# Row statistics: the squares of the last two tiles summed by TensorE instead of GpSimd, and the last output tile in two column halves

## What is computed

```python
def rmsnorm(x, w):
    xf = x.astype(jnp.float32)
    y = xf * lax.rsqrt(jnp.mean(xf * xf, axis=-1, keepdims=True) + EPS)
    return y.astype(x.dtype) * w
...
    for l in range(DEPTH):
        h = rmsnorm(x, norm_w[l])
        proj = h @ w_in[l]
...
        x = x + merged @ w_out[l]
    return rmsnorm(x, final_norm_w)
```

## Time and profile before

| | us |
|---|---|
| median of 3 runs | 3040.17 |
| lowest, highest | 3035.26, 3040.46 |
| span of the profiled execution | 3039.6 |
| TensorE busy in it | 2960.4 (97%) |
| VectorE, ScalarE, GpSimd busy | 1725.0, 1422.3, 421.7 |

### The profile page before, as it was taken

The page is one execution under the profiler, slowest core; times in us unless marked ns, Lnnn a source line. Parts: engine busy times, 40 slices in busy tenths (PEclk is TensorE's granted clock), DMA queues, the critical chain, the costliest instruction groups (busy, mean ns, idle before and its releaser), DMA issues. The chain is left out here.

```text
span 3039.6 us, 51611 instructions
## 1 busy us (share of the span) xinstructions
PE 2960.4 (97%) x20584; PEld 2383.2 (78%) x20584; DVE 1725.0 (57%) x2616; ACT 1422.3 (47%) x2795; POOL 421.7 (14%) x282
## 2 busy tenths in 40 slices
PE   9999989999999999999999999999999999999999
PEld 7788768777787878778777777778888877788887
DVE  7766742677437676733767445554444455554444
ACT  4555542666434555533666345763232356633322
POOL 1554510000013445400000020000000100000000
PEclk9999999999999999999999999999999999999999
DMA  4121112221222112112121222213222221122222
GB/s 151 64 83 59 51 59 89 73 75 60 84 88 98 64 64 85 42 66 91 60 74 60 106 87 87 77 49 111 97 97 97 84 87 62 51 98 98 95 97 83
DMA packets 42688, 243.17 MB, mean 80 GB/s; under 512 B 6832, under 2 KB 7792, under 8 KB 17136
## 3 DMA queue, kind: packets, MB, share of 16 engines
q1 hardware_dynamic: 42480, 240.30, 22.4%
HBM read 233.36 MB, written 2.20 MB: 77 GB/s over the span
## 5 line engine op out<-in xcount | busy, mean ns | idle before, releaser
L319 PE MATMUL bank<-hT,ws 128*128 128x512 f32 x2112 | 873.5, 414 | 12.7 <-issue 7.2
L323 PE MATMUL bank<-hT,ws 128*128 128x512 f32 x2112 | 827.5, 392 | 0.0
L322 PE MATMUL bank<-hT,ws 128*128 128x512 f32 x2112 | 825.9, 391 | 0.0
L319 PEld LDWEIGHTS bank<-hT,ws 128*128 128x128 f32 x2112 | 398.2, 189 | 96.9 <-issue 18.5
L276 DVE TENSOR_TENSOR ws<-raw,ws 128x2048 fp32r<-128x2048 f32 x160 | 372.7, 2330 | 164.7 <-ACT ws L270 161.6
L323 PEld LDWEIGHTS bank<-hT,ws 128*128 128x128 f32 x2112 | 397.3, 188 | 87.3
L270 ACT ACTIVATE ws<-raw 128x2048 fp32r<-128x2048 f32 x172 | 328.8, 1912 | 290.8 <-PE bank L319 175.5
L322 PEld LDWEIGHTS bank<-hT,ws 128*128 128x128 f32 x2112 | 399.0, 189 | 68.1 <-issue 1.4
L1113 PE MATMUL bank<-uS,ws 128*128 128x512 f32 x512 | 199.2, 389 | 0.0
L1116 PE MATMUL bank<-uS,ws 128*128 128x512 f32 x512 | 199.2, 389 | 0.0
L1117 PE MATMUL bank<-uS,ws 128*128 128x512 f32 x512 | 199.2, 389 | 0.0
(11 more groups left out here) (382 smaller groups left out, 4859.2 us busy)
## 6 DMA issues: line engine op xcount, KB each, us to landing
raw<-in_w_ff SPq DMA_DIRECT2D x64, 1024.0 KB, 4.7
raw<-in_w_delta SPq DMA_DIRECT2D x32, 1024.0 KB, 4.7
raw<-in_w_diff SPq DMA_DIRECT2D x32, 1024.0 KB, 4.7
raw<-in_w_att SPq DMA_DIRECT2D x20, 1024.0 KB, 4.8
raw<-in_w_merge_a SPq DMA_DIRECT2D x16, 1024.0 KB, 4.8
raw<-in_w_merge_b SPq DMA_DIRECT2D x16, 1024.0 KB, 4.8
raw<-in_w_out SPq DMA_DIRECT2D x16, 1024.0 KB, 4.8
rows<-sum_rows SPq DMA_DIRECT2D x16, 512.0 KB, 5.6
```

The lines of the kernel that those rows point to most:

```text
L319: first = pe.matmul(out, hi, x[:, 0, k], start=(begin and k == steps[0]), stop=False)
L322: pe.matmul(out, hi, x[:, 1, k], start=False, stop=False)
L323: last = pe.matmul(out, lo, x[:, 0, k], start=False, stop=(end and k == steps[-1]))
```

## The change

The square of tile 6 gets a buffer of its own (`sq[:, 2]`), and so does that of tile 7 (`sq[:, 3]`). GpSimd adds tiles 1 to 5 only (`GATHERED` = 6). `gathered_sum` sums `sq[:, 0]` as before and then tile 6's square, by two more matmuls. The last tile of `k.xT` is made, added and squared in two column halves: TensorE runs its product twice over 256 columns, into two banks (`last_half`, `LAST_BANKS_FF`), and VectorE adds each half as it is done. In the last feed-forward panel of either layer it is the same, and at the kernel's end the last tile is written out by two transfers. With two norms, the gate weights' raw copy moves to another buffer, since the squares now need its place.

```diff
+GATHERED = KT - 2
+SQUARES = 4
 class RowTotals(RowStats):
...
-    def square(self, act, t):
-        if t >= 2:
+    def square(self, act, t, added=None, before=0):
+        if 2 <= t < GATHERED:
             act.wait_ge(self.gathered, t - 1)
-        for part in HALVES if t == KT - 1 else (slice(0, SEQ),):
-            act.activation(self.sq[:, min(t, 1), part], self.k.xT[:, t, part], ACT.Square,
+        for j, part in enumerate(HALVES) if t == KT - 1 else ((0, slice(0, SEQ)),):
+            if added is not None:
+                act.wait_ge(added, before + t + 1 + j)
+            act.activation(self.sq[:, min(t, 1) + max(t + 1 - GATHERED, 0), part], self.k.xT[:, t, part], ACT.Square,
                            scale=1.0 if self.gain is None else self.gain[:, t:t + 1]).then_inc(self.squared, 1)
...
-        for t in range(1, KT - 1):
+        for t in range(1, GATHERED):
             self.gather_one(pool, t)
...
     def gathered_sum(self, pe):
-        pe.wait_ge(self.gathered, KT - 2)
+        pe.wait_ge(self.gathered, GATHERED - 1)
         for j, part in enumerate(HALVES):
             pe.matmul(self.half(j), self.k.ones, self.sq[:, 0, part], start=True, stop=False)
+        pe.wait_ge(self.squared, KT - 1)
+        for j, part in enumerate(HALVES):
+            pe.matmul(self.half(j), self.k.ones, self.sq[:, 2, part], start=False, stop=False)
...
             pe.wait_ge(self.squared, KT + j)
-            pe.matmul(self.half(j), self.k.ones, self.sq[:, 1, part], start=False, stop=True).then_inc(self.summed, 1)
+            pe.matmul(self.half(j), self.k.ones, self.sq[:, 3, part], start=False, stop=True).then_inc(self.summed, 1)
...
-    def square(self, act, t):
-        self.first.square(act, t)
+    def square(self, act, t, added):
+        self.first.square(act, t, added)
         if t == 0:
...
     def gather(self, pool):
-        for t in range(1, KT - 1):
+        for t in range(1, GATHERED):
             self.first.gather_one(pool, t)
...
                 pe.wait_ge(self.added, n - banks[n - 1::-1].index(banks[n]))
-            whole(st.product(pe, k.bank[banks[n]][:, :], c, h, self.aS)).then_inc(self.tile, 1)
+            if n < KT - 1:
+                whole(st.product(pe, k.bank[banks[n]][:, :], c, h, self.aS)).then_inc(self.tile, 1)
+                continue
+            for j, part in enumerate(HALVES):
+                if j:
+                    pe.wait_ge(self.added, KT - 2)
+                whole(st.product(pe, self.last_half(j), c, h, self.aS[:, :, :, part])).then_inc(self.tile, 1)
+    def last_half(self, j):
+        return self.k.bank[self.banks[(KT - 1, KT - 3)[j]]][:, HALVES[j]]
...
         def square(n):
-            act.wait_ge(self.added, n + 1)
             if self.unscaled:
+                act.wait_ge(self.added, n + 1 + n // (KT - 1))
                 self.unscaled.high(act, n)
-            stats.square(act, n)
+            stats.square(act, n, self.added)
         act.preload_act_table_set(LN_EXP)
...
         def add(n):
-            dve.wait_ge(self.tile, n + 1)
-            dve.tensor_tensor(k.xT[:, n], k.xT[:, n], k.bank[self.banks[n]][:, :], ALU.add).then_inc(self.added, 1)
+            for j, part in enumerate(HALVES) if n == KT - 1 else ((0, slice(0, SEQ)),):
+                dve.wait_ge(self.tile, n + 1 + j)
+                dve.tensor_tensor(k.xT[:, n, part], k.xT[:, n, part], self.last_half(j) if n == KT - 1 else k.bank[self.banks[n]][:, :], ALU.add).then_inc(self.added, 1)
             if self.unscaled:
...
-    out = OutStage(k, st, following, aS, sq[:, 0:2], banks + banks, left, pairs, gate_weights, late=True)
+    out = OutStage(k, st, following, aS, sq[:, 0:SQUARES], banks + banks, left, pairs, gate_weights, late=True)
     fn_loaded, = k.sems("final_gain_loaded")
-    norms = TwoNorms(k, out.stats, gain, fn_loaded, sq[:, 2:4], 6)
+    norms = TwoNorms(k, out.stats, gain, fn_loaded, sq[:, SQUARES:2 * SQUARES], 6)
     with k.nc.Block() as block:
...
+LAST_BANKS_FF = (7, 3)
 OUT_BANKS_FF = (0, 1, 2, 3, 6, 2, 3, 6)
...
         rr = k.sb(ctx, "row_scale", [P, SEQ], F32)
-        stats = RowTotals(k, k.sb(ctx, "sq", [P, 2, SEQ], F32), 0) if following else None
+        stats = RowTotals(k, k.sb(ctx, "sq", [P, SQUARES, SEQ], F32), 0) if following else None
         with nc.Block() as block:
...
                     for n in range(KT):
-                        sp.wait_ge(added, nth(NP - 1, 8, n + 4))
-                        sp.dma_start(result[:, n], k.xT[:, n]).then_inc(stored, 16)
-                    sp.wait_ge(stored, 16 * KT)
+                        for j, part in enumerate(HALVES) if n == KT - 1 else ((0, slice(0, SEQ)),):
+                            sp.wait_ge(added, nth(NP - 1, 8, n + 4 + j))
+                            sp.dma_start(result[:, n, part], k.xT[:, n, part]).then_inc(stored, 16)
+                    sp.wait_ge(stored, 16 * (KT + 1))
...
-                    def step(kk, n):
+                    def step(kk, n, part=slice(0, SEQ), bank=None):
                         if kk == 0:
...
                             pe.wait_ge(added, nth(i, 8, (c - 2) * 4 + n))
-                        o = k.bank[4 + n][:, :]
+                        o = k.bank[4 + n if bank is None else bank][:, part]
                         hi, lo = (w[:, kk, n * P:(n + 1) * P] for w in wv)
-                        first = pe.matmul(o, hi, uS[:, 0, kk], start=(kk == 0), stop=False)
+                        first = pe.matmul(o, hi, uS[:, 0, kk, part], start=(kk == 0), stop=False)
                         if kk == 0 and n == 0:
                             first.then_inc(st.slot_free, 1)
-                        pe.matmul(o, hi, uS[:, 1, kk], start=False, stop=False)
-                        last = pe.matmul(o, lo, uS[:, 0, kk], start=False, stop=(kk == 3))
+                        pe.matmul(o, hi, uS[:, 1, kk, part], start=False, stop=False)
+                        last = pe.matmul(o, lo, uS[:, 0, kk, part], start=False, stop=(kk == 3))
                         if kk == 3:
...
                     if last_panel and c == 3:
-                        for n in range(4):
+                        for n in range(3):
                             for kk in range(4):
                                 step(kk, n)
+                        for j, part in enumerate(HALVES):
+                            if j:
+                                pe.wait_ge(relu, 4 + 4 * NP)
+                            for kk in range(4):
+                                step(kk, 3, part, LAST_BANKS_FF[j])
                         if stats:
...
                     last.then_inc(tile, 1)
-                pe.wait_ge(out.added, KT)
+                pe.wait_ge(out.added, KT + 1)
                 inner(0, 1)
...
                                 act.wait_ge(added, nth(i, 8, n + 4))
-                                stats.square(act, n)
+                                if n < KT - 1:
+                                    stats.square(act, n)
+                                else:
+                                    stats.square(act, n, added, nth(i, 8, 4) - 1)
                                 if n == 4:
...
                     for n in range(4 * (c - 2), 4 * (c - 1)):
-                        dve.wait_ge(otile, nth(i, 8, n))
-                        dve.tensor_tensor(k.xT[:, n], k.xT[:, n], k.bank[4 + n % 4][:, :], ALU.add).then_inc(added, 1)
+                        for j, part in enumerate(HALVES) if last and n == KT - 1 else ((0, slice(0, SEQ)),):
+                            dve.wait_ge(otile, nth(i, 8, n + j))
+                            dve.tensor_tensor(k.xT[:, n, part], k.xT[:, n, part], k.bank[LAST_BANKS_FF[j] if last and n == KT - 1 else 4 + n % 4][:, part], ALU.add).then_inc(added, 1)
                         if last and following and n == 5:
...
```

More of the change, by code:

```diff
@@ L1006, in _ @@
             norms.vector(dve, rows)
-            dve.wait_ge(out.added, KT)
+            dve.wait_ge(out.added, KT + 1)
     k.next_phase()
@@ L3450, in build @@
                         if more:
[L3451 removed]
+                            out_phase(k, s_out, s_next, mS, macc[:, 0:SQUARES], OUT_BANKS_MERGE, KT - 1, [(pA, a["pA"][l + 1])],
                                       weights(split, a["gA"], l + 1))
@@ L3456, in build @@
                         first_split = split_area(yS, NGATE)
-                        raw = Carve(macc[:, 4], F32)(KT, NGATE)
+                        raw = Carve(k.cb[:, CB_N:], F32)(KT, NGATE)
                         last_out_phase(k, s_out, s_next, mS, macc, OUT_BANKS_MERGE, KT - 1, a["fn"], gain, pB[:, 0, PB_N1:PB_N1 + KT],
@@ L3477, in build @@
                     k.sb(two, "before_uS", [P, 32 if more else 128], F32)
-                    out_ff_phase(k, s_out, yS, k.sb(two, "sq", [P, 2, SEQ], F32), OUT_TILE[TILES - 1],
+                    out_ff_phase(k, s_out, yS, k.sb(two, "sq", [P, SQUARES, SEQ], F32), OUT_TILE[TILES - 1],
                              s_ff, s_next, lambda t, l=l: pB[:, l, PB_N2 + t:PB_N2 + t + 1],
```

1 line of the change is left out of this document (removed).

## The result

The changed kernel takes 3042.70 us (median of 13 runs, 3037.79 to 3044.72), the kernel before 3036.54 us (13 runs, 3034.20 to 3040.86, among them the three shown ahead of the prediction). The ratio is 1.0016, 95% interval [1.0009, 1.0024]: 0.16% slower, within the 0.2% that the prediction calls no change. Eleven more runs (e10) beside 27 more of before gave 3042.14 against 3039.46 us, ratio 1.0012 [1.0003, 1.0022].

What follows compares the result with a forecast made beforehand. TensorE's queue, 97% busy, was taken as the bound. Terms 0.63 + 2.02 + 2.34 - 0.37 - 0.22 = +4.40 us on 3040.17 gave 3044.6 us, 0.14% slower; range 3037.8 to 3048.5 us.

Steps and rivals of the forecast that it cites:

- D: End of layer 0's feed-forward part: the 1.1 us GpSimd stall goes, passes take back two thirds; -0.37 us.
- The price of a half-width matmul: Each 256-column matmul of the last tile's product: 0.120 us, bounded below by 0.112 us from idle products.
- w: Time added to a projection's last-tile product by making it as 48 half-width matmuls: +0.32 us.
- A: End of block 1's output projection, layer 0: last sums start later, TensorE not ready for early squares; +0.63 us.
- B: End of block 1's output projection, layer 1, two norms: eight passes added to a full queue; +2.02 us.
- C: Block 2's output projection, layer 0: four more passes and a longer product in a full queue; +1.17 us.
- E: Block 2's output projection, layer 1: four more passes and a longer product in a full queue; +1.17 us.
- w': Time added to a feed-forward tile's product, 12 matmuls when whole, by making it in halves: +0.16 us.
- The pass: One of two TensorE passes in each 256-column float32 sum over the partitions: 0.213 us; two sums cost 0.85 us.
- F: Kernel's end: shorter last addition -0.28 us, smaller output write about -0.1 us, longer product w'; together -0.22 us.
- Rival 1: Half-width products: uncovered weight loads give 3061 us, a milder form 3046 to 3049; chance 0.18, 0.04 for full price.
- Rival 2: In A, B, D and F the addition-squares-last-sum chain sets the end, so earlier squares gain: -3 us, 3037; chance 0.07.

Runs made afterwards that it cites:

- e10: The changed kernel run again unaltered, beside the kernel before: median 3042.14 against 3039.46 us, ratio 1.0012.
- e4: The kernel before with one more GpSimd addition ahead of tile 6's (two in B): profiled span 3041.2 us, places' sum +2.3 us against before.
- e7: The changed kernel with the last feed-forward tile in quarters of 128 columns (D and F): profiled span 3049.3 us, places' sum +9.1 us against before.
- e1: The changed kernel with the last tile whole again, only the sums moved to TensorE: profiled span 3040.4 us, places' sum +3.1 us against before.
- e2: The changed kernel with GpSimd adding tile 6 again, only the column halves kept: profiled span 3036.4 us, places' sum +0.3 us against before.
- e3: The changed kernel without the eight idle products ahead of D's sums: profiled span 3037.0 us, D -1.13 us against before.

## Why the prediction was right

Forecast 3044.6 us, measured 3042.7, from a base that itself moved from 3040.17 to 3036.54.

- *The bound* (TensorE's queue; GpSimd waited for only in D): right, and e4 measured it: GpSimd had 1.3 us or more to spare everywhere but in D.
- *The price of a half-width matmul*, 0.120 us: right wherever it can be read off (w came to 0.31 in A and B and 0.34 in C and E, w' to 0.155 in D). It was composed from a stream and an amount on top, and e7 shows that this picture ends just below: by it a quarter would take 0.067 us and it takes 0.111. The lower bound that the prediction took from the idle products was the true floor.
- *The pass*, 0.213 us: 0.216 in place of it, 0.07 us over the 24 passes of the 12 added sums.
- *A*: right within 0.08 us, for the reason given (TensorE isn't ready for the early squares); e1 and e2 show the slack that both parts use. *B, C, E*: right. *D*: right, the passes and idle products take what the stall gave; e3 shows the second of them.
- *F*: mis-sized by 0.12 us. The addition saved 0.27 and w' cost 0.16, as told; the smaller write saved 0.22 us, from its issue to the span's end 4.67 us for 4.89, where the sum had 0.1. In e4, with before's code there, the same stretch is 5.01 us, so 0.1 us of it is what executions differ by.
- *Left out of the sum*: the landing of the weights in C and E. The prediction has no term for it, not even among those "at nothing", and the two traces of the changed kernel show 0.7 and 1.3 us.
- *The base*: the number that was furthest off. 3040.17 is the median of three runs, of which two lay at the upper end; the median of 13 is 3036.54, 3.6 us lower, as the low end of the range allowed for. The two medians then differ by 6.2 us, 1.8 more than the 4.40 that were added, and so the forecast came out only 1.9 us high. That closeness is luck, two errors against each other; the places are not.
- *Span and time*: the profiled execution's own time isn't its span. In every profiled run with both numbers the time is 1.7 to 1.8 us above the span (3042.7 and 3040.9; 3040.1 and 3038.3 for another run of before), so the profiled execution of before took some 3041.4 us, an estimate, and was a long one of its kind. No number of the forecast hangs on it.
- *The figures set aside*: the 262 and 518 cycles that the prediction calls a weight-load figure are, on the page "TensorE: Matmul & The Clock Gate" of the Trainium skill, section "Back-to-back issue gap", spacings of matmuls. By them w would be -0.20 us, an estimate; it came to +0.31 to +0.34, so it was right to leave them out.
- *"Its clock granted nearly in full all along"* was true to a tenth and hid what decides the spread.
- *Rival 1* (the weight load shows) fell in both forms: no half-width product came to more than 0.121 us a matmul. *Rival 2* (the early squares are the path) fell for the change, though for A and F by themselves it holds: e2 gains 0.32 and 0.34 us there.

## What to carry to other kernels

When an engine is 97% busy, taking work off an idle neighbour is worth only the waits that the full engine has for it: list those waits first (here one, of 1.1 us), and make the edit there and nowhere else. Each pass moved to the full engine costs its full length wherever its queue has no gap, and two edits that use the same gap can't both be credited with it. Measure such a small change place by place, from an anchor that it doesn't touch: two executions of the changed kernel agree within 0.01 us in each place, and only the kernel's end differs by 0.1 us between executions with the same code there, while the totals wander by 7. Then look ahead of the anchors too: here 0.7 to 1.3 us of the price stood there, in loads that landed later.

## What the runs showed that wasn't expected

- Stretches of 3.41 us in which TensorE's clock is granted at half, one to four in the body of an execution, some 1.7 us each. They come and go, but always in the same five parts of the program; 19 of 29 come shortly after TensorE stood still, ten in the midst of matmuls that had followed each other for 7 us. The changed kernel's two executions have them at 446 and 2459 us, and at 390 and 448 us.
- A floor of 0.111 us between matmuls that each load 128 columns of weights, at 128 columns of stream; 0.120 at 256 and 0.2267 at 512.
- A float32 sum of 256 columns costs two passes of 0.216 us, a rounded one a single pass of 0.12 us: 3.6 times less.
- A 16 KB packet of the instruction queue that runs while a weight chunk is under way goes with a landing 0.7 to 1.5 us later, in nine landings of nine, and puts up to 0.5 us of wait into TensorE's queue. Only kernels with the column halves in C and E, which add some 260 instructions, have such packets there.
